# Values of two query blocks in one group, another order of the first transfers, and three output blocks per step in the last unit

## The chip, the core and the metric

The kernel runs on one core of one Trainium2 chip. The metric is the device time of the whole program in microseconds (us), the median of several executions. One further execution was recorded by the hardware profiler; all durations below are from it.

## What is computed

The reference is a three-layer transformer stack on one sequence of 512 tokens with a model width of 1024, all in float32. Cut to what matters here:

```python
# layer a: gMLP + attention over 256 memory rows, then a convolutional FFN
h = rmsnorm(x, a_norm1);  z = h @ a_w_in            # u | v | q_mem
u, vv, q_mem = gelu(z[:768]), gelu(z[768:1536]), z[1536:]
tok = u * spatial_gating(rmsnorm(vv))               # (GMLP blocks of 128)
x = x + concat(tok, memory_attention(q_mem, mem)) @ a_w_out
x = x + conv_ffn(rmsnorm(x))
# layer b: forgetting attention (12 heads of 64, causal, decay) + memory attention
x = x + concat(forgetting_attention(q, k, v, log_f_cum), memory_attention(...)) @ b_w_out
x = x + conv_ffn(rmsnorm(x))
# layer c: stick-breaking attention (8 heads) + differential attention (4 heads)
x = x + gate * (concat(sb_out, df_out) @ w_out_2)

# every softmax attention, for each block i of 128 queries and each head:
p = softmax(q_i @ k.T)          # logits, max, exp, normalisation
o_i = p @ v                     # needs p transposed: keys on the partitions
```

## The kernel before

Everything is kept transposed (features on the 128 partitions, 512 tokens on the free axis). Each large product is made of two float32r parts, high and low, so that one 128x128 weight block costs three TensorE matmuls: high x high, high x low, low x high (`blocks`, lines 380 to 398; `out_block`, lines 1808 to 1810). I call these three matmuls a block, and eight of them (one output tile) a job. A weight chunk comes by DMA into `raw` (two slots, SyncE's queue), ScalarE rounds it into `wh` (`split_hi`, line 300), VectorE subtracts to get `wl` (`split_lo`, line 306), and TensorE counts `w_used` when it is done with it. SyncE loads a chunk into a slot when VectorE has finished with the slot's last one (`w_lo`).

**The order of the work** is written out by hand on each engine, with semaphores between the engines. There is no scheduler.

**The start.** TensorE first runs 20 matmuls on a zeroed tile `warm` (line 1760). Then `value_group(0)` computes the first half of the v projection: for each of the eight 128-row slices k of x, twelve matmuls of 384 columns (lines 1700 to 1702), into four PSUM banks. Slice k needs `xh` and `xl` of that slice (ScalarE lines 444 and 445, VectorE lines 452 to 456; the squares for the norm are summed on the way, in `sq` and `acc`) and the weight chunk that holds slice k. The chunks of group 0 hold slices (0), (1), (2, 3, 4), (5, 6, 7) (`VSETS`). Ahead of slice 7 stand the sums of the squares over the partitions (`x_sums`, lines 1709 and 1715). SyncE issues par, chunk 0, x slice 0, chunk 1, x slice 1, x slices 2 and 3, chunk 2, x 4 and 5, x 6 and 7, chunk 3, and then constants and the memory rows.

**The softmax units.** Two heads share a unit. Ten units use `two_pe`, `two_act` and `two_dve`: `ma` 0 and 1 (memory attention of layer a), and in layer b `mb` 0, `fx` 0, `fx` 1, `mb` 1, `fx` 2 to 5 (`UNITS`). A unit has ten steps t (`pe_pairs`). In even steps TensorE does `logits(t/2)` of a query block (line 483, weights of 64 rows; for `fx` a mask matmul, line 540) and `turned` of the block before (line 547, transposes of the probabilities, 128 rows and columns). In each step it then does `between(t)`, a share of the projection jobs of the next unit: `FILL` gives 3, 3, 2, 2, 2, 3, 3, 0 jobs for the eight units of layer b, and the last unit of layer b does blocks of `b_out` instead. In steps 3, 5, 7, 9 it ends with `values(i)` for i = 0, 1, 2, 3 (line 559, weights of 64 columns). ScalarE's `copy` takes the transposes out of PSUM into `pta` or `ptb`, which has one half for each head. The first `values` of an `fx` unit also waits for `b_vn`: the values of this unit, transposed at t = 2 (line 436) and copied by ScalarE into `vnb`.

**The last unit** of the program (u = 7, differential attention) has its own copies of these steps (logits line 483, turns line 2020, values line 2032). No projection is left, so `between_last` puts blocks of the last product, `c_out`, there: `OUT_EARLY` lists 42 of them, and `OUT_FROM` gives how many are done by the start of each step: 2, 2, 2, 3, 2, 2, 2, 3, 2, 2. The others come after the unit.

Of the kernel before, what the change touches and what calls it, by code (L numbers as in the profile page):

```python
# [12 lines left out]
P = 128  # L13
D = 1024
S = 512
# [17 lines left out]
STAGES = [("front", 23, 14), ("a_out", 8, 8), ("a_f1", 44, 44), ("a_f2", 16, 8),  # L33
# [9 lines left out]
VSETS = (((0, 1), (1, 1), (2, 3), (5, 3)), ((0, 3), (3, 3), (6, 2)))  # L43
FRONT = ([("v", 0, i) for i in range(4)] + [("v", 1, i) for i in range(3)] +
# [3 lines left out]
FRONT_UNIT = [range(17, 20), range(20, 23)]  # L48
# [28 lines left out]
def build(nc, t, decay, out):  # L77
    with ExitStack() as ctx:
# [53 lines left out]
        minus = sb("minus", [P, 2 * P], F32R)  # L132
# [37 lines left out]
        pta = at("pta", [P, 2, MEM], F32, 24)  # L170
        vn = at("vn", [P, TT, TOKW], F32, 52)
        warm = at("warm", [P, S], BF16, 52)
# [12 lines left out]
        ptb = at("ptb", [P, 2, S], F32, 78)  # L185
# [11 lines left out]
        aws = at("aws", [P, 2, S], F32, 50)  # L197
        sgs = at("sgs", [P, S], F32, 56)
# [34 lines left out]
        x_hi, x_lo = sem("x_hi"), sem("x_lo")  # L233
        s_sum, s_root, s_r = sem("s_sum"), sem("s_root"), sem("s_r")
# [254 lines left out]
        def pe_pairs(logits, turned, values, between, behind_first=False):  # L489

            for t in range(PE_STEPS):
# [10 lines left out]
                if odd and i >= 1:  # L502
                    values(i - 1)
# [25 lines left out]
        def two_pe(pe, a, it, p, pt, q, k, v, nk, decayed, o_free, between, ready=None):  # L529
# [20 lines left out]
            def values(i):  # L550
# [6 lines left out]
                for b in range(last + 1):  # L557
                    for h in range(2):
                        mm = nc.tensor.matmul(ob[heads(h), i * P:(i + 1) * P], v(h, b), pt[:, h, b * P:(b + 1) * P],  # L559
                                              start=(b == 0), stop=(b == last))  # L560
# [126 lines left out]

        def front_width(n):
# [35 lines left out]
        def _(sp):  # L724
# [28 lines left out]
            def load_x(m):  # L753
                k = [i for i in range(KD) if XPART[i] == m]
                sp.dma_start(xt[:, k[0]:k[-1] + 1, :], t["x_t"][:, k[0]:k[-1] + 1, :]).then_inc(in_x[m], 16)
# [12 lines left out]
            for m in range(2):  # L768
                sp.dma_start(memt[:, 4 * m:4 * m + 4, :], t["mem_t"][:, 4 * m:4 * m + 4, :]).then_inc(in_mem[m], 16)
            load_front(4)  # L770
            sp.dma_start(wsnat[:, :, :], t["ws_t"]).then_inc(in_ws, 16)
            sp.dma_start(kf[:, 2 * P:NKEEP], t["k_tiles"][:, 2 * P:NKEEP]).then_inc(in_c, 16)
            load_front(5)
            sp.dma_start(biast[:, :, :], t["bs_t"]).then_inc(in_bi, 16)
            sp.dma_start(par[:, NROWS:], t["params"][:, NROWS:]).then_inc(in_c, 16)
            load_front(6)
            sp.dma_start(kb[:, :].bitcast(F32), t["k_bf16"]).then_inc(in_kb, 16)
            for n in range(7, len(FRONT)):
                load_front(n)
# [62 lines left out]
        def _(act):  # L842
# [8 lines left out]
            def value_gelu(g, b):  # L851
# [3 lines left out]
                else:  # L855
                    act.wait_ge(w_used, (4, 7)[g])
# [9 lines left out]

            table(EXP_LN_SET)
            act.wait_ge(in_par, 16)
            front_hi(0)
            for k in range(KD):  # L870
                x_hi_part(act, X0["a_in"], k, k % 2, col("a_norm1", k), xh, in_x[XPART[k]], 16)
                if k in (0, 2, 4):
                    front_hi(k // 2 + 1)
            front_hi(4)
            act.wait_ge(k_set, 1)
# [3 lines left out]
            front_hi(5)  # L879
# [8 lines left out]
            front_hi(6)  # L888
            front_hi(7)
            for b in range(TT):  # L890
                value_gelu(1, b)
            table(EXP_LN_SET)
            front_hi(8)
            factor(s_sum, 1, rmem[:, :], zb[0][:, :MEM], s_root, s_r)
            factor(c_sum, 1, sm[:, 56:58], zb[0][:, 260:262], c_root, c_rec)
            front_hi(9)
# [3 lines left out]
            for n in range(10, 19):  # L900
                front_hi(n)

            def behind_front(u):

                def f(t):
                    for n in FRONT_UNIT[u]:
                        if unit_end(u, n) + 1 == t and n < 21:
# [9 lines left out]
            def rest_front(u):  # L917
                mix_high(act, 6 + u, u, ob[:, :], att["ma"]["pv"], 8 * u + 8)
                for n in FRONT_UNIT[u]:
                    if unit_end(u, n) + 1 >= PE_STEPS - 1 and n < 21:  # L920
# [267 lines left out]
        def _(dve):  # L1188
# [34 lines left out]
            nc.vector.memset(warm[:, :], 0.0).then_inc(k_warm, 1)  # L1223
# [950 lines left out]
```

## Time and profile before

| | us |
|---|---|
| median of 3 executions | 1458.16 (1457.49 to 1461.1) |
| the profiled execution | 1456.96 |
| its span, first to last instruction | 1455.2 |
| TensorE matmuls busy | 1444.9 |
| VectorE busy | 961.2 |
| ScalarE busy | 670.1 |
| granted TensorE clock, mean | 1.00 of full |

A matmul's row gives its start and a modelled duration that overlaps the next matmul's start. So what a matmul costs is read from start to start: a 128x512 matmul of a block has a row of 0.39 us and the next one starts 0.23 us later. "Idle before" in brackets is time in which an engine ran nothing, with what ended it.

### The profile page before, as it was taken

To read this page: it belongs to the slowest core of one execution; us is meant where nothing else is said; L and a number is where in the kernel's file an instruction comes from. 1 tells how busy PE (TensorE), PEld (TensorE's weight loads), DVE (VectorE), ACT (ScalarE), POOL (GpSimd) and SP (SyncE) were. 2 spreads that over 40 slices of the span, in tenths; PEclk is the share of its full clock that TensorE was granted. 3 is DMA by queue.
4 is the path that set the end of the run, shared out by engine and by line. 5 is a ranking of instruction groups with operands and counts; after the bars stand their busy time and mean duration, and the time that the engine had idled before them with its cause. 6 is when DMAs were issued, how large, how long until landed. Compare 5 with 4: busy or idle time off the path is not lost.

```text
span 1455.2 us, 20045 instructions
## 1 busy us (share of the span) xinstructions
PE 1444.9 (99%) x7052; PEld 1152.1 (79%) x7052; DVE 961.2 (66%) x1581; ACT 670.1 (46%) x1104; POOL 41.2 (3%) x82
## 2 busy tenths in 40 slices
PE   9999999999999999999999999999999999999999
PEld 8977888888888887777778888888888877777777
DVE  5656777777766647555457777777677666666773
ACT  7435444444442234444454444444323366665661
POOL 0000000000001110000000000000111000000000
PEclk9999999999999999999999999999999999999999
DMA  6323222332247733212132323323676511112222
GB/s 226 129 89 117 73 88 100 101 98 90 101 143 232 241 107 116 74 59 88 59 102 67 106 86 101 101 88 117 202 243 232 166 51 59 58 58 73 73 74 87
DMA packets 44301, 162.66 MB, mean 112 GB/s; under 512 B 5060, under 2 KB 5700, under 8 KB 44240
## 3 DMA queue, kind: packets, MB, share of 16 engines
q1 hardware_dynamic: 33984, 126.70, 26.0%
q0 software_dynamic: 9104, 33.06, 6.8%
q10 hardware_dynamic: 1152, 2.10, 0.4%
q8 instruction: 37, 0.61, 0.2%
q14 instruction: 24, 0.20, 0.0%
HBM read 159.72 MB, written 2.12 MB: 111 GB/s over the span
## 4 chain that ended last, share of the span: by engine, by line
PE 95%; DVE 2%; ACT 1%; DMA 1%; issue 0%; SPq 0%; DVEq 0%; ACTq 0%
PE ps L380 17%; PE ps L382 17%; PE ps L381 17%; PE ps L396 6%; PE ps L398 6%; PE ps L397 6%; PE ps L1808 3%; PE ps L1810 3%; PE ps L1809 3%; PE ps L483 2%; PE ps L559 2%; PE ps L547 2%; PE ps L1986 2%; PE ps L1742 1%; PE ps L1744 1%; PE ps L1743 1%
## 5 line engine op out<-in xcount | busy, mean ns | idle before, releaser
L306 DVE TENSOR_TENSOR wl<-raw,wh 128x1024 fp32r<-128x1024 f32 (+3 forms) x198 | 253.7, 1281 | 122.9 <-ACT wh L300 122.8
L300 ACT CAST wh<-raw 128x1024 fp32r<-128x1024 f32 (+3 forms) x198 | 217.5, 1098 | 228.0 <-PE ps L382 194.8
L380 PE MATMUL ps<-xh,wh 128*128 128x512 f32 x720 | 281.1, 390 | 0.6 <-DVE hb L1366 0.6
L382 PE MATMUL ps<-xh,wl 128*128 128x512 f32 x720 | 280.1, 389 | 0.0
L381 PE MATMUL ps<-xl,wh 128*128 128x512 f32 x720 | 280.1, 389 | 0.0
L380 PEld LDWEIGHTS ps<-xh,wh 128*128 128x128 f32 x720 | 135.2, 188 | 29.5 <-issue 2.0
L381 PEld LDWEIGHTS ps<-xl,wh 128*128 128x128 f32 x720 | 135.2, 188 | 28.5 <-issue 0.5
L382 PEld LDWEIGHTS ps<-xh,wl 128*128 128x128 f32 x720 | 135.2, 188 | 28.3
L396 PE MATMUL ps<-xh,wh 128*128 128x512 f32 x344 | 144.8, 421 | 0.0
L380 PE MATMUL ps<-hth,wh 128*128 128x512 f32 x352 | 136.9, 389 | 0.0
L381 PE MATMUL ps<-htl,wh 128*128 128x512 f32 x352 | 136.9, 389 | 0.0
L382 PE MATMUL ps<-hth,wl 128*128 128x512 f32 x352 | 136.9, 389 | 0.0
L398 PE MATMUL ps<-xh,wl 128*128 128x512 f32 x344 | 134.8, 392 | 0.0
L397 PE MATMUL ps<-xl,wh 128*128 128x512 f32 x344 | 134.3, 390 | 0.0
L970 ACT CAST hth<-hid 128x512 f32 (+1 forms) x44 | 27.3, 621 | 136.6 <-DVE hid L1378 136.6
L963 ACT ACTIVATE ct<-hb,par 128x512 f32<-128x512 f32 x88 | 71.8, 816 | 34.2 <-DVE hb L1366 34.0
L1366 DVE TENSOR_TENSOR hb<-ps,rbc 128x512 f32<-128x512 f32 x88 | 60.5, 688 | 38.8 <-PE ps L382 38.7
L396 PEld LDWEIGHTS ps<-xh,wh 128*128 128x128 f32 x344 | 64.9, 189 | 15.4 <-issue 3.7
L381 PEld LDWEIGHTS ps<-htl,wh 128*128 128x128 f32 x352 | 66.1, 188 | 13.8
L380 PEld LDWEIGHTS ps<-hth,wh 128*128 128x128 f32 x352 | 66.1, 188 | 13.8
L382 PEld LDWEIGHTS ps<-hth,wl 128*128 128x128 f32 x352 | 66.1, 188 | 13.5
L398 PEld LDWEIGHTS ps<-xh,wl 128*128 128x128 f32 x344 | 64.6, 188 | 14.6
(300 smaller groups left out, 2347.7 us busy)
## 6 DMA issues: line engine op xcount, KB each, us to landing
raw<-w_a_f SPq DMA_DIRECT2D x44, 512.0 KB, 3.2
raw<-w_b_f SPq DMA_DIRECT2D x44, 512.0 KB, 3.2
row<-w_c_rows POOLq DMA_DIRECT2D x32, 512.0 KB, 4.6
row<-w_ada_rows POOLq DMA_DIRECT2D x24, 512.0 KB, 4.8
raw<-w_a_f SPq DMA_DIRECT2D x16, 704.0 KB, 4.0
raw<-w_b_f SPq DMA_DIRECT2D x16, 704.0 KB, 4.2
raw<-w_b_pair SPq DMA_DIRECT2D x18, 512.0 KB, 3.3
raw<-w_front SPq DMA_DIRECT2D x16, 512.0 KB, 3.2
```

The lines of the kernel that those rows point to most:

```text
L300: nc.scalar.copy(wh[:, s, :width], raw[:, s, :width]).then_inc(w_hi, 1)
L306: nc.vector.tensor_tensor(wl[:, s, :width], raw[:, s, :width], wh[:, s, :width].bitcast(F32), ALU.subtract).then_inc(w_lo, 1)
L380: nc.tensor.matmul(dst, a, h(k), start=(k == 0), stop=False)
L381: nc.tensor.matmul(dst, a, l(k), start=False, stop=False)
L382: mm = nc.tensor.matmul(dst, b, h(k), start=False, stop=(k == total - 1))
L396: nc.tensor.matmul(dst[:, :], a, h(r), start=(k == 0), stop=False)
L397: nc.tensor.matmul(dst[:, :], a, l(r), start=False, stop=False)
L398: mm = nc.tensor.matmul(dst[:, :], b, h(r), start=False, stop=(k == KD - 1))
L963: nc.scalar.activation(ct[:, l, :], hb[:, l, 2:], ACT.Identity, bias=w(3), scale=w(2)).then_inc(f_c0, 1)
L1366: nc.vector.tensor_tensor(hb[:, l, 2:], po[(J0[L + "_f1"] + l) % 2][:, :], rbc[:, :], ALU.mult).then_inc(po_free, 1)
L1808: nc.tensor.matmul(dst[:, :], a, MIX[0](r), start=(k == 0), stop=False)
L1809: nc.tensor.matmul(dst[:, :], a, MIX[1](r), start=False, stop=False)
```

## The change

Three things are changed.

1. `values` of query blocks 0 and 1 are both done at the end of step 5, those of 2 and 3 at the end of step 9 (`pv_at`), in the ten units of `two_pe`. The copied transposes have two buffers (`pta[i % 2]`, `ptb[i % 2]`), and `copy` waits for the values of two query blocks earlier. `minus` moves elsewhere in SBUF to make room.
2. The start: 9 matmuls on `warm` and not 20. x slice 0 is loaded from ScalarE's queue, chunk 0 is the first on SyncE's queue, then par, x slice 1, chunk 1; x slices 2 and 3 are issued when x slice 0 is there. The chunks hold slices (0), (1), (2), (3, 4), (5, 6, 7), one chunk more, so all numbers behind it rise by one. `xh` of slice 0 is made by VectorE. Slice 0's twelve matmuls are ordered by part (`first_products`). The squares are taken two slices at a time into `sqx` and added in pairs.
3. In the last unit three blocks of `c_out` are done in each step (`OUT_FROM`), 30 in all and not 22. Behind the unit 9 blocks, and not 8, stand ahead of the k = 7 blocks of the first four output tiles.

```diff
-STAGES = [("front", 23, 14), ...
+STAGES = [("front", 24, 14), ...
-VSETS = (((0, 1), (1, 1), (2, 3), (5, 3)), ((0, 3), (3, 3), (6, 2)))
+VSETS = (((0, 1), (1, 1), (2, 1), (3, 2), (5, 3)), ((0, 3), (3, 3), (6, 2)))
...
-        def pe_pairs(logits, turned, values, between, behind_first=False):
+        def pe_pairs(logits, turned, values, between, behind_first=False, pv_at={1: (0,), 2: (1,), 3: (2,), 4: (3,)}):
...
-                if odd and i >= 1:
-                    values(i - 1)
+                if odd and i in pv_at:
+                    for e in pv_at[i]:
+                        values(e)
...
-            pe_pairs(logits, turned, values, between)
+            pe_pairs(logits, turned, values, between, pv_at={2: (0, 1), 4: (2, 3)})
...
-                wait(act, a["pv"], 8 * it + s - 1)
-                nc.scalar.copy(pt[:, s % 2, :n], turn_bank(a, it, s)[:, :n]).then_inc(a["copy"], 1)
+                wait(act, a["pv"], 8 * it + s - 3)
+                nc.scalar.copy(pt[s // 2 % 2][:, s % 2, :n], turn_bank(a, it, s)[:, :n]).then_inc(a["copy"], 1)
...
+            load_front(0)
             sp.dma_start(par[:, :NROWS], t["params"][:, :NROWS]).then_inc(in_par, 16)
-            load_front(0)
-            load_x(0)
+            load_x(sp, 1)
             load_front(1)
-            load_x(1)
-            load_x(2)
+            sp.wait_ge(in_x[0], 16)
+            load_x(sp, 2)
             load_front(2)
-            load_x(3)
-            load_x(4)
             load_front(3)
+            load_x(sp, 3)
+            load_x(sp, 4)
+            load_front(4)
...
+            dve.wait_ge(in_par, 16)
+            dve.wait_ge(in_x[0], 16)
+            nc.vector.tensor_scalar(xh[:, 0, :], xt[:, 0, :], col("a_norm1", 0), None, ALU.mult).then_inc(x_hi, 1)
             front_lo(0)
...
+            first_add(1)
             front_lo(4)
+            first_lo(6)
+            first_lo(7)
+            first_add(2)
+            first_add(3)
+            dve.wait_ge(x_add, 3)
+            nc.vector.tensor_tensor(acc[:, :], sqx[:, 0, :], sqx[:, 1, :], ALU.add).then_inc(x_add, 1)
...
+            def first_products():
+                a, b = wh[:, 0, :VW], wl[:, 0, :VW]
+                for s_in, part, w in ((w_hi, xh, a), (w_lo, xh, b), (x_lo, xl, a)):
+                    pe.wait_ge(s_in, 1)
+                    pe.wait_ge(x_hi, 1)
+                    for i in range(TT):
+                        mm = nc.tensor.matmul(vbank[0][i][:, :VW], part[:, 0, i * P:(i + 1) * P], w,
+                                              start=(part is xh and w is a), stop=False)
+                mm.then_inc(w_used, 1)
...
-            for _ in range(20):
+            for _ in range(9):
                 nc.tensor.matmul(st[:, :], warm[:, 0:P], warm[:, :], start=True, stop=True)
...
-            OUT_FROM = [0, 2, 4, 6, 9, 11, 13, 15, 18, 20, 22]
+            OUT_FROM = [3 * t for t in range(PE_STEPS + 1)]
...
-            for i in range(23, 31):
+            for i in range(31, 40):
```

On ScalarE, at the start of the program before the change (`wh<-raw` is a weight chunk, `sq<-xt` and `xh<-xt` are the square and the high part of one x slice):

```order
1 L466 ACT_TABLE_LOAD
2 L300 CAST wh<-raw 128x384
3 L444 ACTIVATE sq<-xt 128x512
4 L445 ACTIVATE xh<-xt,par 128x512
5 L300 CAST wh<-raw 128x384
6 L444 ACTIVATE sq<-xt 128x512
7 L445 ACTIVATE xh<-xt,par 128x512
8 L444 ACTIVATE sq<-xt 128x512
9 L445 ACTIVATE xh<-xt,par 128x512
10 L300 CAST wh<-raw 128x1152
```

And after it (`sqx` takes the squares of two slices at once):

```order
1 L694 DMA xt<-x_t 128x512
2 L469 ACT_TABLE_LOAD
3 L303 CAST wh<-raw 128x384 x2
4 L448 ACTIVATE xh<-xt,par 128x512 x3
5 L303 CAST wh<-raw 128x384
6 L877 ACTIVATE sqx<-xt 128x1024
7 L303 CAST wh<-raw 128x768
8 L448 ACTIVATE xh<-xt,par 128x512 x2
9 L877 ACTIVATE sqx<-xt 128x1024
10 L303 CAST wh<-raw 128x1152
```

The high part of slice 0 has left ScalarE, both first chunks stand ahead of every x slice, and the squares stand behind the slices that they belong to.

On TensorE, in unit `fx` 1 of layer b before the change: the end of step 7, the start of step 8, and further down the end of step 9 with the logits of the next unit (L559 are the values, L547 the turns, L396 to L398 a block):

```order
1477 L398 MATMUL ps<-xbh,wl 128x512
1478 L559 MATMUL ps<-ptb,vnb 64x128 x6
1479 L547 MATMUL ps<-kf,pb 128x128 x8
1480 L396 MATMUL ps<-xbh,wh 128x512
...
1491 L398 MATMUL ps<-xbh,wl 128x512
1492 L559 MATMUL ps<-ptb,vnb 64x128 x8
1493 L483 MATMUL ps<-kmb,qmr 128x256 x2
```

And the same places after it (L563 the values, L551 the turns, L399 to L401 a block):

```order
1468 L401 MATMUL ps<-xbh,wl 128x512
1469 L551 MATMUL ps<-kf,pb 128x128 x8
1470 L399 MATMUL ps<-xbh,wh 128x512
...
1481 L401 MATMUL ps<-xbh,wl 128x512
1482 L563 MATMUL ps<-ptb_113,vnb 64x128 x6
1483 L563 MATMUL ps<-ptb_69,vnb 64x128 x8
1484 L486 MATMUL ps<-kmb,qmr 128x256 x2
```

The six values matmuls of query block 2 have moved from between a block and the turns to the end of the unit, where they stand directly ahead of those of block 3.

## Rows read from the trace of the kernel before

**Rows 1.** First part of the page: busy us, share of the span, instructions

```profile
PE 1444.9 (99%) x7052; PEld 1152.1 (79%) x7052; DVE 961.2 (66%) x1581; ACT 670.1 (46%) x1104; POOL 41.2 (3%) x82
```

**Rows 2.** Waits of PE, longest in total: us in total, times, longest

```profile
PE ps L2020 <- DVE pd L1661: 1.7, 2, 1.1
```

**Rows 3.** Timeline of PE and its weight loads, start: start us, us, engine, line

```profile
4.15 0.15 PEld L1760 LDWEIGHTS ps<-warm 128*128 128x128 bf16 x1 [0.28 <-issue]
4.49 1.39 PEld L1760 LDWEIGHTS ps<-warm 128*128 128x128 bf16 x7 [0.19 <-issue]
...
7.40 0.41 PE L1700 MATMUL ps<-wh,xh 128*128 128x384 f32 x1 [0.16 <-DVE xl L456]
...
12.49 0.44 PE L1700 MATMUL ps<-wh,xh 128*128 128x384 f32 x1 [0.29 <-DVE wl L306]
...
23.02 0.95 PE L1709 MATMUL ps<-kf,acc 128*128 128x1 f32 x8
```

**Rows 4.** Timeline of SP's queue, ACT and DVE, from the start

```profile
1.66 0.42 SPq L755 DMA_DIRECT2D xt<-x_t  x1
...
4.90 0.63 ACT L444 ACTIVATE sq<-xt 128x512 f32<-128x512 f32 x1 [0.48 <-DMA xt<-x_t]
...
6.51 0.74 DVE L456 SCALAR_TENSOR_TENSOR xl<-xt,par,xh 128x512 fp32r<-128x512 f32 x1
...
14.16 1.16 ACT L300 CAST wh<-raw 128x1152 fp32r<-128x1152 f32 x1 [0.90 <-DMA raw<-w_a_v]
...
15.36 1.36 DVE L306 TENSOR_TENSOR wl<-raw,wh 128x1152 fp32r<-128x1152 f32 x1 [0.20 <-ACT wh L300]
...
35.80 1.23 DVE L1234 TENSOR_TENSOR sqm<-sqm 128x1024 f32<-128x1024 f32 x1 [1.41 <-ACT sqm L886]
```

**Rows 5.** DMA view of the first 40 us: GB/s in each microsecond

```profile
GB/s 0 23 194 278 330 278 364 405 328 376 328 366 414 387 337 417 415 403 407 419 406 290 31 172 322 4 0 0 0 0 0 184 340 0 0 0 0 0 0 0
```

**Rows 6.** Timeline of PE in unit fx 1 of layer b

```profile
615.32 0.40 PE L398 MATMUL ps<-xh,wl 128*128 128x512 f32 x1
616.24 0.44 PE L559 MATMUL ps<-ptb,vnb 128*64 128x128 f32 x4 [0.52 <-issue]
616.61 0.92 PE L483 MATMUL ps<-kr,qr 64*128 64x384 f32 x4
...
620.78 1.13 PE L483 MATMUL ps<-kr,qr 64*128 64x512 f32 x4
...
624.47 0.39 PE L398 MATMUL ps<-xbh,wl 128*128 128x512 f32 x1
624.79 0.88 PE L559 MATMUL ps<-ptb,vnb 128*64 128x128 f32 x12
625.60 1.09 PE L547 MATMUL ps<-kf,pb 128*128 128x128 f32 x8
626.45 0.48 PE L396 MATMUL ps<-xbh,wh 128*128 128x512 f32 x1
```

**Rows 7.** Timeline of ACT and DVE in the same unit

```profile
615.58 0.56 ACT L1009 COPY vnb<-ps 128x512 f32<-128x512 f32 x1
```
```profile
625.26 0.48 DVE L608 TENSOR_SCALAR pb<-pb,sm 128x512 f32<-128x512 f32 x1
```

**Rows 8.** Timeline of PE in the last unit

```profile
1412.07 0.55 PE L2020 MATMUL ps<-kf,pd 128*128 128x128 f32 x3 [0.66 <-DVE pd L1661]
1412.37 0.48 PE L1808 MATMUL ps<-mixh,wh 128*128 128x512 f32 x1
...
1415.90 0.83 PE L2032 MATMUL ps<-ptd,vns 128*128 128x128 f32 x6
1417.80 0.66 PE L2020 MATMUL ps<-kf,pd 128*128 128x128 f32 x4 [1.07 <-DVE pd L1661]
```

**Rows 9.** Timeline of ACT and DVE in the last unit

```profile
1414.53 0.73 ACT L1159 ACTIVATE pd<-pd,sm 128x512 f32<-128x512 f32 x1
```
```profile
1416.99 0.75 DVE L1661 SCALAR_TENSOR_TENSOR pd<-pd,sm 128x512 f32<-128x512 f32 x1
```

More of the change, by code:

```diff
@@ L686, in leftover, with load_x @@
                     project(jobs[0] + j)
+        def load_x(eng, m):
+            k = [i for i in range(KD) if XPART[i] == m]
+            eng.dma_start(xt[:, k[0]:k[-1] + 1, :], t["x_t"][:, k[0]:k[-1] + 1, :]).then_inc(in_x[m], 16)
         def front_width(n):
@@ L865, in factor, with first_hi, first_squares @@
                 nc.scalar.activation(dst, dst, ACT.Exp, scale=-0.5).then_inc(s_out, 1)
+            def first_hi(k):
+                x_hi_part(act, X0["a_in"], k, k % 2, col("a_norm1", k), xh, in_x[XPART[k]], 16, square=False)
+            def first_squares(e):
+                p = (0, 1, 2, 1)[e]
+                nc.scalar.activation(sqx[:, 2 * p:2 * p + 2, :].rearrange("p a n -> p (a n)"),
+                                     xt[:, 2 * e:2 * e + 2, :].rearrange("p a n -> p (a n)"), ACT.Square).then_inc(x_sq, 1)
+            load_x(act, 0)
             table(EXP_LN_SET)
+            front_hi(0)
+            front_hi(1)
             act.wait_ge(in_par, 16)
[L869 to L873, printed above, removed]
-            front_hi(4)
+            act.wait_ge(x_hi, 1)
+            for k in (1, 2, 3):
+                first_hi(k)
+            front_hi(2)
+            first_squares(0)
+            front_hi(3)
+            first_hi(4)
+            first_hi(5)
+            first_squares(1)
+            front_hi(4)
+            first_hi(6)
+            first_hi(7)
+            first_squares(2)
+            act.wait_ge(x_add, 1)
+            first_squares(3)
+            front_hi(5)
             act.wait_ge(k_set, 1)
@@ L899, in _ @@
             factor(v_acc, 0, sm[:, 12:16], sm[:, 12:16], v_root, v_r, TOKW)
-            for n in range(10, 19):
+            for n in range(11, 20):
                 front_hi(n)
@@ L1248, in _ @@
             dve.wait_ge(s_r, 1)
-            for n in range(7, 17):
-                if n == 8:
+            for n in range(8, 18):
+                if n == 9:
                     dve.wait_ge(s_r, 2)
-                if n == 11:
+                if n == 12:
                     dve.wait_ge(c_rec, 2)
@@ L1255, in _ @@
                 front_lo(n + 2)
-                if n in (7, 9):
-                    for k in range(4 * (n == 9), 4 * (n == 9) + 4):
+                if n in (8, 10):
+                    for k in range(4 * (n == 10), 4 * (n == 10) + 4):
                         dve.wait_ge(m_hi, 8 + k + 1)
@@ L1688, in value_group @@
                     s = n % 2
+                    if n == 0:
+                        first_products()
+                        continue
                     pe.wait_ge(w_lo, n + 1)
@@ L1764, in _ @@
             value_group(1, mem_sums)
-            for n in range(7, 17):
-                if n < 9:
-                    pe.wait_ge(v_gelu, n - 2)
+            for n in range(8, 18):
+                if n < 10:
+                    pe.wait_ge(v_gelu, n - 3)
                 front_chunk(n)
@@ L2043, in _ @@
                 out_block("c_out", j, KD - 1)
-            for i in range(31, 42):
+            for i in range(40, 42):
                 out_block("c_out", *OUT_EARLY[i])
```

77 lines of the change are left out of this document (45 added, 32 removed).

## The prediction

> **What bounds the kernel now.** I read the page first: TensorE is busy 99% of the span, VectorE 66%, ScalarE 46% [rows 1]. So a change can only gain where TensorE starts late, waits, or pays something between two groups of matmuls that the busy figure hides. The view of TensorE's waits has little to give: the largest entry is 1.7 us in two waits of the last unit [rows 2]. What is hidden shows only in the timeline, read from start to start. There are three places, and the change touches each: the first 23 us [rows 3, 4], the joints of the attention units [rows 6], and the last unit [rows 8].
>
> **Values in pairs.** Read the end of step 7 in unit `fx` 1 [rows 6]. A block's last matmul starts at 624.47, and the values follow 0.32 later, where a block's matmuls follow each other every 0.23. The 12 values matmuls take 0.81 until the turns start. With 128 columns each at the pace that a 512-column matmul has (0.23 / 4, at best 0.053), 12 take 0.64. So 0.17 of the group is fixed. The group of 4 in step 3 takes 616.61 - 616.24 = 0.37 against 0.21: again 0.16 fixed. A values group uses 64 columns of weights, the logits 64 rows, all else 128 by 128: the fixed part is a change of that shape.
>
> - Step 3: the values go, the logits follow the block directly. The entry of 0.32 stays (it is then the logits'), 0.16 goes.
> - Step 7: the values go, and turns (128 by 128, as the block) follow the block. 0.17 goes, the entry falls by 0.09, and the turns' own 0.85 for 8 transposes probably loses some 0.05 of the same kind: 0.31.
> - Steps 5 and 9: the second group follows the first in the same shape: nothing.
>
> That is 0.47 a unit, and 4.7 us for ten units. The lower bound, if only the step-3 kind of saving holds at both places, is 3.2; the upper one, if a group's whole entry goes too (0.25 and 0.40), is 6.5. I take 4.7, the value read in the place itself.
>
> A second gain: in `fx` 1 the first values wait. From 615.32 to 616.24 are 0.92 us where 0.32 is normal, and 616.24 is just behind ScalarE's copy into `vnb`, which runs from 615.58 for 0.56 [rows 6, 7]. "Issue" in the brackets is thus a wait for `b_vn`. The other unit that begins with two jobs, `fx` 2, has the same shape. With the values in step 5 this copy is two steps old: 2 x 0.60 = 1.2 us gone.
>
> A new cost: what is removed was cover. The turns of step 8 need VectorE's normalisation of block 3, whose chain starts at logits(3) (620.78). The second of its two halves (two heads) ends at 625.26 + 0.48 = 625.74, 4.96 behind the logits [rows 6, 7]. TensorE would reach the turns now at 624.47 + 0.23 = 624.70, 3.92 behind the logits, and not at 625.60. The last four of the eight transposes wait until 625.8 and, at 0.1 each (0.85 / 8), end near 626.2, where without a wait all would be done at 625.5. That is 0.7 us of new wait. `fx` 2 has the same two jobs behind it, `mb` 1 too, with 256 columns and so a shorter chain; I put it at half, 0.4. Sum 1.8. In the units with three jobs a step holds 2.4 blocks and not 1.6; over two steps that is 1.1 us more cover (a block is 3 x 0.23), and 1.0 us is what is lacking. So I book nothing there, but it is close. The looser wait of `copy` (the second buffer) costs nothing, and step 4's turns lose 0.37 to 0.6 of cover, which in `fx` 1 the removed wait shows they have, since the turns stand behind the logits of 616.61 by 0.85 and more.
>
> Attention: -4.7 - 1.2 + 1.8 = **-4.1 us**. Bounds -6 (no new wait) and -2.
>
> **The start.** TensorE's first real product starts at 7.40 [rows 3]; it waited for `xl` of slice 0, whose chain began when x slice 0 came at 4.90 [rows 4]. Slice 0 was the third transfer on SyncE's queue, issued at 1.66, two slots of 0.42 behind the first [rows 4]; now it is the first on ScalarE's, 0.9 us earlier, so it comes near 4.0. VectorE makes `xh`, `wl` and `xl` in at most 0.74 each, the time of `xl`: all by 6.2, and `first_products` needs `xl` only for its last four matmuls, 8 x 0.175 behind its start. So TensorE starts it when the 9 warm matmuls end. Their weight loads are 0.43 apart up to 4.15, and from 4.49 seven fit in 1.39 [rows 3]; the ninth ends near 4.8. That alone would give 2.6 us. But the products must then be fed. The last chunk of group 0 (slices 5 to 7) came at 14.16 and its `wl` was done at 15.36 + 1.36 = 16.72 [rows 4]. What is transferred up to and with it is the same before and after: par (55 KB), eight x slices of 256 KB, eight slices of weights of 192 KB, 3639 KB or 3.73 MB. The stream reaches that sum at 13.1 us [rows 5], a microsecond before the cast, so it is the volume that sets the landing, and no order of issue changes it. Slice 5 can then not start before 16.8. Before, it ran near 12.49 + 3 x 2.1 = 18.8 (slices 2 to 6 and nothing else lie between 12.49 and 23.02: 60 matmuls at 0.175). The gain is 2.0, and `x_sums` comes at 16.8 + 4.2 = 21.0 and not 23.0. VectorE's sum of squares ends there as well: behind `wl` at 16.7 come two `xl` (1.5), two adds of 1024 columns (1.23 each) and one of 512 (about 0.7), near 21.3, or 21.0 with the overlap of successive rows. Everything behind hangs on TensorE's progress and moves with it.
>
> The Trainium skill ("DMA: Bandwidth & Descriptors", Specifications) gives 435 GB/s as the ceiling of the transfers into SBUF; the busiest microsecond here shows 419 [rows 5], so the trace comes near it, but the mean from 2 to 13 us is 333. By that rule the chunk could land 2 us earlier, VectorE's chain would set `x_sums`, and the gain would be 2.8.
>
> Start: **-2.0 us**. Bounds -2.8 (the chunk lands 0.8 earlier) and -0.5 (one of the now tighter steps, chunk 2 behind x slices 2 and 3 above all, costs 1.5).
>
> **The last unit.** TensorE waits 0.66 before the turns of block 2 and 1.07 before those of block 3 [rows 8]. Both are for VectorE's normalisation, and TensorE's work behind the unit is the same whatever stands inside. A block takes 0.70 (five between 1412.37 and 1415.90). By step 6 five more blocks have been done, of which two lie between logits(2) and the turns of block 2: 1.4 against a wait of 0.66. Between the turns of block 2 and of block 3 there are six blocks, not five. The chain behind logits(3) is set by ScalarE, whose exponential starts at 1414.53 and leads to `pd` at 1416.99 + 0.75 = 1417.74 [rows 9]. It starts when ScalarE has done its list for the step, and this list moves by two blocks (1.4), TensorE by six (4.2) less the 0.66 won: 1.4 - 4.2 + 0.66 = -2.1 against 1.07. Both waits go: **-1.7 us**. The new waits that are possible are for the weights of output tiles 2, 3 and 4 (made in steps 3, 5, 7, read first in steps 4, 7, 9) and for the mixed row of unit 6, read from step 6 on. By their distances they are met with 1 us and more to spare, since TensorE is the one that comes later. Bounds -1.8 and 0.
>
> **The sum.** -4.1 - 2.0 - 1.7 = **-7.8 us**. The profiled execution took 1456.96 and would take 1449.2; it lies 1.2 below the median of the runs, 1458.16, so I predict 1450.4.
>
> **Rivals.**
>
> 1. *New waits eat the attention's gain.* If the normalisation is late by 0.7 us at step 8 in all ten units, attention is -4.7 - 1.2 + 7 = +1.1, and the total -2.6: 1455.6. For it: the three-job units have only about 0.1 us to spare by my count. Against: memory units have chains of 256 columns, and the first `fx` units of three jobs show no wait now. Chance 0.12.
> 2. *The start doesn't move.* TensorE starts early but stands for the chunks, and gains nothing by slice 5: -5.8, 1452.4. For it: 3639 KB is a fixed volume. Against: before, slice 5 ran 2 us behind its weights. Chance 0.08.
> 3. *Slower: the slow pace comes back.* The weight loads show that the array runs at half pace (1.2 GHz) up to the eighth warm matmul, then at 2.4 [rows 3]. Nine matmuls leave one or none at the fast pace. If the clock rises later, or falls in a gap while slices 1 and 2 wait, a product of 384 columns costs 0.32 and not 0.17; from 53 of the 96 products of group 0 on this outweighs 7.8 us, and with all 96 the time is 1458.16 - 7.8 + 14.4 = 1464.8. Against: a gap of 0.5 us ahead of 12.49 brought no slow product, and 12 products a slice keep the array busy. The Trainium skill ("TensorE: Matmul & The Clock Gate", Part 1) says the slow state is the default, that activity releases it, and that the moment varies by some 0.5 us from run to run. A shift of 0.5 us would make three products slow, 0.5 us. Chance 0.03.
> 4. *The edit of the last unit does nothing* (the chains move with the blocks): -6.1, 1452.1. Chance 0.05.
>
> The forecast keeps 0.72. A measurement of this kernel can tell about 0.3% (4.4 us) from no change. Faster by more than that: the forecast and rivals 2 and 4 less their outliers, 0.82; within 0.3%: rival 1 and a part of the rest, 0.14; slower: rival 3 and what I don't see, 0.04. The range: the best bounds sum to -10.6, the worst to -2.5; I take 1447.0 to 1455.0.
>
> **What would show it.** In the new trace: the first product near 4.8; slice 5 near 16.8 and the sums of squares near 21.0; no entry for values in steps 3 and 7, and turns directly behind a block; in `fx` 1 and 2 a wait of TensorE for `pb` at step 8 of about 0.5 that wasn't there, and none for `vnb`; no wait for `pd` in the last unit. The prediction is wrong if such waits for `pb` stand in all `fx` units, if slice 5 starts later than 17.5, or if 384-column products 0.32 apart stand behind the warm ones.

## The result and the profile after

The changed kernel takes 1450.09 us (median of 5 runs, 1449.13 to 1451.27), the kernel before 1458.16 (1457.49 to 1461.1, also of 5). The ratio is 0.9944, with a 95% interval of 0.9932 to 0.9955: 8.1 us faster, where 7.8 were forecast. The profiled execution took 1451.27, the longest of the five, with a span of 1449.5; that of before, 1456.96, is below each of those five. So the two traces differ by 5.7 us only. What is missing to 8.1 lies at the start and in what follows from it, as the table below shows.

The head of the page and the waits of TensorE (us in total, times, longest us), to be held against [rows 1, 2]:

```profile
PE 1438.8 (99%) x7041; PEld 1151.6 (79%) x7041; DVE 961.8 (66%) x1579; ACT 669.5 (46%) x1100; POOL 41.0 (3%) x82
```
```profile
PE ps L1753 <- DVE wl L309: 2.2, 2, 1.3
...
PE ps L551 <- DVE pb L612: 0.7, 2, 0.3
PE ps L399 <- DVE wl L309: 0.7, 1, 0.7
...
PE ps L486 <- ACT pb L579: 0.6, 2, 0.3
PE ps L1806 <- DVE wl L309: 0.4, 1, 0.4
```

The wait for `pd`, 1.7 us before, is gone. Two waits for `pb` at the turns are new, as forecast. But 2.2 us of waits for weights in group 0 (L1753) and 0.7 in a unit of stage `sb` (L399) are new as well, and neither was booked.

The start of TensorE after (start us, us, engine, line; against [rows 3]):

```profile
4.98 0.94 PE L1766 MATMUL ps<-wh,xh 128*128 128x384 f32 x4 [0.31 <-DVE xh L1261]
...
7.54 0.41 PE L1753 MATMUL ps<-wh,xh 128*128 128x384 f32 x1 [0.23 <-DVE xl L459]
10.78 0.44 PE L1753 MATMUL ps<-wh,xh 128*128 128x384 f32 x1 [0.90 <-DVE wl L309]
18.57 0.44 PE L1753 MATMUL ps<-wh,xh 128*128 128x384 f32 x1 [1.27 <-DVE wl L309]
23.18 1.02 PE L1772 MATMUL ps<-kf,acc 128*128 128x1 f32 x8
```

The first product comes at 4.98 (4.8 was forecast), 2.4 earlier than before. Yet slice 5 starts at 18.57, behind 1.27 of waiting, and the sums at 23.18: in this execution nothing is left of the head start. The queue of SyncE, ScalarE and VectorE show why (against [rows 4]), and the DMA view of the first 40 us shows where the transfers dip (against [rows 5]):

```profile
10.76 0.33 SPq L759 DMA_DIRECT2D raw<-w_a_v  x1
```
```profile
15.97 1.16 ACT L303 CAST wh<-raw 128x1152 fp32r<-128x1152 f32 x1 [0.59 <-DMA raw<-w_a_v]
```
```profile
17.16 1.36 DVE L309 TENSOR_TENSOR wl<-raw,wh 128x1152 fp32r<-128x1152 f32 x1 [0.52 <-ACT wh L303]
```
```profile
GB/s 0 39 217 385 331 138 331 285 257 366 379 325 189 355 282 258 324 410 424 385 415 399 370 278 61 120 351 21 0 0 0 106 381 37 0 0 0 0 0 0
```

The load of the last chunk is issued at 10.76, because it waits for the slot that chunk 2 leaves, and VectorE ends chunk 2 at 10.7. The microseconds from 5, from 8 and from 12 move 138, 257 and 189 GB/s, where before none from 3 to 14 us was under 278; the one from 12 follows on a stretch from 7.9 to 10.76 in which SyncE issues nothing. By 14 us 3.60 MB had come, and before 4.07. This is one execution: in `mixed`, a kernel below with the same code up to the first unit, 3.83 MB had come by then.

In unit `fx` 1 (against [rows 6]) the values of blocks 0 and 1 are one group of 12, and the turns of step 8 come straight behind a block, but late:

```profile
616.61 0.40 PE L401 MATMUL ps<-xbh,wl 128*128 128x512 f32 x1
616.94 0.88 PE L563 MATMUL ps<-ptb,vnb 128*64 128x128 f32 x12
617.75 1.13 PE L486 MATMUL ps<-kr,qr 64*128 64x512 f32 x4
...
621.44 0.39 PE L401 MATMUL ps<-xbh,wl 128*128 128x512 f32 x1
622.17 1.25 PE L551 MATMUL ps<-kf,pb 128*128 128x128 f32 x8 [0.35 <-DVE pb L612]
623.18 0.48 PE L399 MATMUL ps<-xbh,wh 128*128 128x512 f32 x1
```

Nothing waits for `vnb` any more: the values start 0.33 behind their block, and not 0.92. From the block to the end of the turns are 0.73 + 1.01 = 1.74; in the units of three jobs, where nothing waits, it is 0.23 + 0.79 = 1.02. So the new wait costs 0.72, twice the 0.35 that its row shows. A row counts idle time from the modelled end of the block's last matmul, 0.16 behind the point where the next one would have started (0.39 against 0.23): that makes 0.50 ahead of the group. The other 0.22 lies inside the group, whose second four transposes wait for VectorE's second half, and the merged row hides it. In the last unit (against [rows 8]) both turns follow without a wait:

```profile
1411.08 0.55 PE L2084 MATMUL ps<-kf,pd 128*128 128x128 f32 x3
...
1415.37 0.39 PE L1874 MATMUL ps<-mixh,wl 128*128 128x512 f32 x1
1415.60 0.83 PE L2096 MATMUL ps<-ptd,vns 128*128 128x128 f32 x6
1416.26 0.60 PE L2084 MATMUL ps<-kf,pd 128*128 128x128 f32 x4
```

### The profile page after: what moved, and what is told of

Its sections match the earlier page's. It is cut to its first block, busy times and chain, and to the rows that moved or that the text cites. A ratio compares the mean times of both kernels' runs of the same rounds, so it can differ in the third digit from the quotient of the medians.

```text
span 1449.5 us, 20006 instructions
## 1 busy us (share of the span) xinstructions
PE 1438.8 (99%) x7041; PEld 1151.6 (79%) x7041; DVE 961.8 (66%) x1579; ACT 669.5 (46%) x1100; POOL 41.0 (3%) x82
## 4 chain that ended last, share of the span: by engine, by line
PE 93%; DVE 4%; DMA 2%; ACT 1%; issue 1%; POOL 0%; ACTq 0%; DVEq 0%; POOLq 0%
PE ps L383 17%; PE ps L384 17%; PE ps L385 17%; PE ps L399 5%; PE ps L401 5%; PE ps L400 5%; PE ps L1872 3%; PE ps L1874 3%; PE ps L1873 3%; PE ps L486 3%; PE ps L563 2%; PE ps L2050 1%; PE ps L551 1%; PE ps L1806 1%; PE ps L1808 1%; DVE wl L309 1%
## 5 line engine op out<-in xcount | busy, mean ns | idle before, releaser
L399 PE MATMUL ps<-xh,wh 128*128 128x512 f32 x344 | 144.5, 420 | 0.7 <-DVE wl L309 0.7
L401 PE MATMUL ps<-xh,wl 128*128 128x512 f32 x344 | 134.6, 391 | 0.0
L399 PEld LDWEIGHTS ps<-xh,wh 128*128 128x128 f32 x344 | 64.9, 189 | 16.0 <-issue 4.4
L401 PEld LDWEIGHTS ps<-xh,wl 128*128 128x128 f32 x344 | 64.6, 188 | 14.3
```

Source lines behind the costliest of these rows:

```text
L399: nc.tensor.matmul(dst[:, :], a, h(r), start=(k == 0), stop=False)
L401: mm = nc.tensor.matmul(dst[:, :], b, h(r), start=False, stop=(k == KD - 1))
```

## The experiments

Ten other kernels and the changed one once more ran in three groups, each group on one chip with the kernel before beside it (medians 1458.51 for `pairs_only`, `out_only`, `start_only` and `no_start`; 1457.66 for `warm20`, `mem_later`, `early2` and `mixed`; 1458.2 for `step3_only`, `after_again` and `best`). The theory was the sum of the prediction, with the start corrected: the issue of the last chunk's load sets slice 5. To tell parts apart below the resolution of the times, I cut every profiled execution at the same instructions. "Sums" is the start of `x_sums`, "first unit" that of `ma` 0. All in us:

| kernel | median | up to sums | sums to first unit | two `ma` units | `a_out` to `b_qm` | eight layer-b units | to last unit | last unit to end |
|---|---|---|---|---|---|---|---|---|
| before | 1458.16 | 23.02 | 58.42 | 46.92 | 431.98 | 188.23 | 648.47 | 58.16 |
| pairs_only | 1453.93 | 23.95 | 58.23 | 45.95 | 431.98 | 185.30 | 648.34 | 58.15 |
| out_only | 1456.09 | 23.61 | 58.77 | 46.91 | 432.00 | 188.25 | 648.45 | 56.11 |
| no_start | 1452.36 | 23.78 | 58.38 | 45.95 | 431.99 | 185.29 | 648.43 | 56.18 |
| step3_only | 1455.2 | 23.71 | 58.47 | 46.53 | 432.02 | 186.17 | 648.41 | 58.19 |
| start_only | 1456.17 | 22.09 | 56.99 | 46.94 | 432.25 | 188.26 | 648.85 | 58.12 |
| after | 1450.09 | 23.18 | 57.72 | 45.92 | 432.23 | 185.35 | 648.98 | 56.12 |
| after_again | 1450.6 | 23.83 | 56.98 | 45.96 | 432.27 | 185.31 | 649.66 | 56.09 |
| warm20 | 1451.35 | 23.36 | 57.92 | 45.95 | 432.21 | 185.31 | 649.15 | 56.10 |
| mem_later | 1450.26 | 22.77 | 56.96 | 45.92 | 432.21 | 185.31 | 649.21 | 56.12 |
| early2 | 1449.85 | 21.86 | 56.96 | 45.92 | 432.21 | 185.29 | 649.71 | 56.05 |
| mixed | 1448.46 | 21.52 | 56.99 | 45.94 | 432.23 | 184.34 | 649.08 | 56.10 |
| best | 1448.84 | 22.77 | 56.97 | 45.92 | 432.24 | 184.34 | 648.72 | 56.04 |

Five of these traces have the old start and eight the new one. Four of the eight (`start_only`, `after`, `after_again`, `mixed`) have the same code up to the first unit. Where nothing was changed, the two `ma` units, the layer-b units and the last unit repeat within 0.15 us from kernel to kernel. The piece up to the sums doesn't, with either start (23.02 to 23.95, 21.52 to 23.83), nor does, with the new start, the piece up to the last unit.

**One part each.** Three kernels make one part of the change each, and one makes all but the start.

```diff
 # against before
-            pe_pairs(logits, turned, values, between)
+            pe_pairs(logits, turned, values, between, pv_at={2: (0, 1), 4: (2, 3)})
...
-                wait(act, a["pv"], 8 * it + s - 1)
-                nc.scalar.copy(pt[:, s % 2, :n], turn_bank(a, it, s)[:, :n]).then_inc(a["copy"], 1)
+                wait(act, a["pv"], 8 * it + s - 3)
+                nc.scalar.copy(pt[s // 2 % 2][:, s % 2, :n], turn_bank(a, it, s)[:, :n]).then_inc(a["copy"], 1)
...
```

> The kernel before with the values of two query blocks in one group, and nothing else. Theory A (the joints of the attention units pay as read from the two traces: 0.47 us a unit gone, two waits for vnb of 0.6 gone, new waits for pb and the exponentials of 2.1 in the three units with two jobs): -3.8 us against the kernel before. Theory B (the whole difference of the medians that the start does not explain, 2.4 us, sits in the attention too): -6 us or more.

1453.93, ratio 0.9974 (0.9965 to 0.9983). By the medians 4.6 us, with 2.5 to 5.1 as its interval: theory B's 6 or more is out. The segments say -0.97 and -2.93, -3.9 together: theory A's figure. Cut at the first logits of each unit, `fx` 1 loses 0.33 and `fx` 2 0.30, `mb` 1 takes 0.15 more, and the five other layer-b units lose 0.47 to 0.51 each.

```diff
 # against before
-            OUT_FROM = [0, 2, 4, 6, 9, 11, 13, 15, 18, 20, 22]
+            OUT_FROM = [3 * t for t in range(PE_STEPS + 1)]
...
-            out_block("c_out", *OUT_EARLY[22])
+            out_block("c_out", *OUT_EARLY[30])
...
```

> The kernel before with three output blocks in every step of the last unit, and nothing else. Theory A: the two waits for pd of 1.7 us go and nothing replaces them: -1.5 to -1.7 us. Rival: the chains of ScalarE and VectorE move with the blocks and the waits stay in part: 0 to -0.7 us.

1456.09, ratio 0.9985 (0.9976 to 0.9994), 2.4 us by the medians. The last unit loses 2.05 us, more than theory A's 1.5 to 1.7, and the rival is out.

```diff
 # against after
-            pe_pairs(logits, turned, values, between, pv_at={2: (0, 1), 4: (2, 3)})
+            pe_pairs(logits, turned, values, between, pv_at={1: (0,), 2: (1,), 3: (2,), 4: (3,)})
...
-            OUT_FROM = [3 * t for t in range(PE_STEPS + 1)]
+            OUT_FROM = [0, 2, 4, 6, 9, 11, 13, 15, 18, 20, 22]
...
```

> The kernel before with the new start alone (values and output blocks in the old order, the second buffer is kept). Theory A (the profiled execution is typical: slices 5 to 7 wait for their weight chunk, whose load is issued 3 us later than before): -0.5 us, slice 5 starts near 18.6 us. Theory B (the profiled execution was a bad one, the volume of the transfers sets the landing): -2.0 us or more, slice 5 near 16.8 us.

1456.17, ratio 0.9983 (0.9974 to 0.9992), 2.3 us under before by the medians, with 1.2 to 3.8 as its interval. That is theory B's time and not theory A's. Slice 5 starts at 17.48, between the two figures, so neither reason is confirmed.

The diffs of `pairs_only` and `out_only` together:

> The changed kernel without the new start: values in pairs and three output blocks a step on the kernel before. If the parts add up: -5.4 us (-3.8 and -1.6) against the kernel before, and 0.5 us (theory A) or 2.5 us (theory B) slower than the changed kernel, which measured -8.1.

1452.36, ratio 0.9966 (0.9952 to 0.9979): 6.1 us for the two other parts, and with the 8.1 of the whole change 2.0 for the start. The three parts alone give 4.6 + 2.4 + 2.3 = 9.3 by the medians, each with about 1.4 us to either side, against 8.1 for the whole; no interaction can be told from that.

**Where in the attention.** Only the values of blocks 0 and 1 are put together:

```diff
 # against pairs_only
-            pe_pairs(logits, turned, values, between, pv_at={2: (0, 1), 4: (2, 3)})
+            pe_pairs(logits, turned, values, between, pv_at={2: (0, 1), 3: (2,), 4: (3,)})
```

> The kernel before with the second buffer and with only the first two values groups put together: the values of blocks 0 and 1 stand in step 5, those of blocks 2 and 3 stay in steps 7 and 9. This splits the attention's gain by place. Theory (0.16 us for each values group that goes between two blocks of logits, another 0.31 at step 7, two waits of 0.60 for vnb that go with step 3, and new waits of 0.7 before the turns of step 8 that come from the removal at step 7 alone): the ma units lose 2 x 0.16 = 0.3 us (46.9 to 46.6), the layer-b units 8 x 0.16 + 1.2 = 2.5 less a wait of 0.3 to 0.4 for an exponential in mb 1 (188.2 to 186.1), no wait for pb at step 8 in fx 1 and fx 2; about 2.4 us under the kernel before, 1455.5. Rival (the fixed price of a change of shape is the same at both places, 0.24 each): ma units 46.4 and layer b 185.5, 3.3 us under before. A second rival (the vnb wait only moves): layer b 187.3.

1455.2, ratio 0.9981 (0.9972 to 0.999); `ma` 46.53, layer b 186.17: the theory said 46.6 and 186.1, the rival with equal shares 46.4 and 185.5, the second rival 187.3. The time, 3.0 us under before, can't tell them apart (2.4 and 3.3 were expected); the segments can. The units `fx` 1 and `fx` 2 lose 0.73 and 0.71 and the five others 0.13 to 0.21 (`mb` 1 takes 0.21 more): so each wait for `vnb` was worth some 0.55. Step 3 is worth (46.92 - 46.53) / 2 = 0.20 in a unit, step 7 (46.53 - 45.95) / 2 = 0.29; 0.16 and 0.31 were predicted. In `fx` 1 of this kernel the turns of step 8 have no wait, and stand behind the values again:

```profile
623.75 0.39 PE L399 MATMUL ps<-xbh,wl 128*128 128x512 f32 x1
624.07 0.88 PE L561 MATMUL ps<-ptb,vnb 128*64 128x128 f32 x12
624.88 1.09 PE L549 MATMUL ps<-kf,pb 128*128 128x128 f32 x8
625.73 0.48 PE L397 MATMUL ps<-xbh,wh 128*128 128x512 f32 x1
```

So the wait for `pb` comes from the removal at step 7 alone: what was taken out there was cover.

That a joint is paid for the change of shape, and not for any change from one group to another, can be read from groups that don't change it. In after, eight turns (128 by 128) directly behind a block:

```profile
600.70 0.39 PE L401 MATMUL ps<-xh,wl 128*128 128x512 f32 x1
600.94 1.03 PE L551 MATMUL ps<-kf,pb 128*128 128x128 f32 x8
601.73 0.48 PE L399 MATMUL ps<-xh,wh 128*128 128x512 f32 x1
```

They start 0.23 behind the block's matmul, as a matmul of the block would, and take 0.79; behind values of 64 columns they take 0.85. The values of the last unit use all 128 columns: at 1415.60 they too start 0.23 behind a block, and the six of them take 0.66 to the turns, 0.11 each, the pace of the turns themselves. No kernel changed the shape alone, so this stands on rows and not on an experiment.

The next kernel puts the values back as cover only in the three units that lack it, `fx` 1 and 2 and `mb` 1:

```diff
+            PV_AT = {0: {2: (0, 1), 4: (2, 3)}, 2: {2: (0, 1), 3: (2,), 4: (3,)},
+                     3: {1: (0,), 2: (1,), 3: (2,), 4: (3,)}, 4: {2: (0, 1), 3: (2,), 4: (3,)}}
...
-                        between_pe(u), (b_vn, it + 1))
+                        between_pe(u), (b_vn, it + 1), PV_AT.get(u, PV_AT[0]))
```

> The changed kernel where the three units with two jobs behind them keep a separate values group: fx 1 and fx 2 in step 7, mb 1 in steps 3 and 7 as before the change. Theory (removing a group took away cover, and the waits for pb and for the exponential that came cost more than the joints saved there): the two waits for pb of 0.35 and the one for the exponential of 0.3 at these units go, 0.41 us gained in each fx unit and 0.2 in mb 1, 1.0 us in all: 1449.1. Rival (the turns take as long as they do for other reasons than the wait): 1.3 us slower, since the joints come back (0.31 + 0.31 + 0.47) and nothing else changes.

1448.46, ratio 0.9936 (0.9922 to 0.9949), and the layer-b units take 184.34, 1.01 less than after, as the theory says: a wait of 0.72 goes for a joint of 0.29 that comes back, twice, and 0.17 in `mb` 1. The rival, 1.3 slower, is out.

**The start.** Twenty warm matmuls again with everything else as changed, so that TensorE starts as late as before:

```diff
-            for _ in range(9):
+            for _ in range(20):
```

> The changed kernel with 20 warm matmuls, and not 9, so that the first product starts near 7.3 us again and not at 5.0. Theory A (what ends the start last is the weight chunk of slices 5 to 7, whose products began at 17.5 and 18.6 us in two executions; slices 0 to 4 take 10.4 us and would end at 17.8): 0 to 0.5 us slower than the changed kernel, 1450.1 to 1450.6. Theory B (each microsecond of an earlier first product is gained): 2.3 us slower, 1452.4.

1451.35, ratio 0.9952 (0.9938 to 0.9965): 1.3 above after, 0.7 above after_again, with intervals as wide as that. It lies above theory A's range and below theory B's figure, and the times don't decide. In its trace the first product starts at 7.39, slices 0 to 4 run without a gap, the last matmul of slice 4 starts at 18.00, and slice 5 waits until 18.76 for the last chunk. So here, as in after (18.57), it is the chunk that sets slice 5. With the earliest chunk of the four executions of after's start (16.90 in mixed) TensorE would have come 1.3 later than the chunk: 20 warm matmuls cost something in such a draw and nothing in this one.

Two kernels move what could hold the last chunk. In one the mem tiles' two loads stand behind the next weights' load and not ahead of it, in the other chunk 2 is treated ahead of x slice 3, so that its slot is free earlier:

```diff
 # mem_later: on SyncE
+            load_front(5)
             for m in range(2):
                 sp.dma_start(memt[:, 4 * m:4 * m + 4, :], t["mem_t"][:, 4 * m:4 * m + 4, :]).then_inc(in_mem[m], 16)
-            load_front(5)
```
```diff
 # early2; the same for first_lo on VectorE
-            for k in (1, 2, 3):
-                first_hi(k)
+            first_hi(1)
+            first_hi(2)
             front_hi(2)
+            first_hi(3)
```

> The changed kernel with the load of the memory rows (1 MB, needed after 28 us) issued behind the first chunk of group 1 and not ahead of it. Theory A (the chunk of slices 5 to 7 lands 5.2 us after its issue because kf and the memory rows share the transfers with it): it lands up to 1.5 us earlier, slice 5 near 17 us, and the time is 0.5 to 1 us under the changed kernel's 1450.1. Rival (it lands late because it is issued at 10.8, when VectorE has done chunk 2, and behind x slices 4 to 7): no difference.

1450.26, ratio 0.9943 (0.993 to 0.9957): no difference by time. The chunk is cast at 15.56, 4.9 behind its issue, and slice 5 starts at 18.16, within what after's own start does (16.90 to 19.23).

> The changed kernel with chunk 2 rounded and subtracted between slices 2 and 3 on ScalarE and VectorE, not behind slice 3. Theory (issue time counts: the load of slices 5 to 7 waits for VectorE to be done with chunk 2, at 10.8 us): it is issued 0.6 us earlier, slice 2 starts 0.6 earlier on TensorE, slice 5 0.5 earlier, 0.5 us faster than 1450.1. Rival (the volume of the transfers counts): slice 2 earlier, slice 5 as before, no difference.

1449.85, ratio 0.9944 (0.9931 to 0.9958), equal by time. In the trace the load is issued at 10.08, 0.7 earlier than in after, and slice 5 starts at 17.25. That is no proof for the theory: mixed, with the load issued at 10.34 by after's own order, has slice 5 at 16.90.

The changed kernel once more, and then the edits of `mixed`, `mem_later` and `early2` together:

> The changed kernel once more, on the chip of the other runs of this call. Theory: the attention, the last unit and layer a's feed-forward agree with its first trace within 0.1 us (45.9, 185.3, 56.1), and only the time up to the first unit differs, within 79 to 82 us, since there the landing of the transfers decides. Rival (the first trace's 80.9 us of start is this order's own): again 80.9 within 0.2.

1450.6, ratio 0.9949 (0.9936 to 0.9963), and a start of 80.81, within the theory's 79 to 82 and at the rival's number, 80.9 within 0.2, too. But start_only and mixed, whose code up to here is the same, have 79.08 and 78.51, so the rival is out, and the theory's range was too narrow below. The agreement with after is a coincidence of two pieces that moved against each other: the sums came at 23.83, not 23.18, and the way from there to the first unit took 56.98, not 57.72.

> The changed kernel with the three edits together that looked best alone: the values of blocks 2 and 3 apart again in the units where their removal brought a wait, the fifth weights chunk's load issued ahead of the mem tiles, and x slice 3 treated behind chunk 2 on ScalarE and VectorE. Theory (the issue of the last chunk's load, gated by chunk 2's two halves, sets slice 5): the load is issued near 10.1 us, slice 5 starts at 16.9 to 17.5, the layer-b units take 184.3, and the time is 1.6 to 2.4 us under the changed kernel of the same call, about 1448. Rival (the volume sets it): slice 5 as in the changed kernel, and only the 1.0 us of the attention.

1448.84, ratio 0.994 (0.9926 to 0.9953): 1.8 under after_again, no better than mixed alone. The time lies in the theory's 1.6 to 2.4, but not for its reason. The load was issued at 9.99, earliest of all, and yet it was cast at 15.55 only, and slice 5 started at 18.16, where 16.9 to 17.5 was expected. That was a miss for the theory:

```profile
9.99 0.33 SPq L759 DMA_DIRECT2D raw<-w_a_v  x1
```
```profile
15.55 1.16 ACT L303 CAST wh<-raw 128x1152 fp32r<-128x1152 f32 x1 [0.31 <-DMA raw<-w_a_v]
```

All thirteen traces side by side give what stands of it. With the old order the last chunk's load is issued at 7.59 to 7.76 and cast at 14.16 to 14.74, within 0.6 us. With the new order it is issued at 9.99 to 11.06 and cast at 14.30 to 16.63, 4.0 to 5.9 behind the issue, and slice 5 follows at 16.90 to 19.23. With the old order this chunk never mattered: its low part was done by 16.7 to 17.4, and TensorE came to slice 5 at 18.9 to 19.8. What set the old start was the chunk of slices 2 to 4, cast at 9.84 to 10.84, whose low part TensorE waits for in all five traces, until 12.49 to 13.44; the trace of before that the prediction read was the earliest of them. With the new order TensorE waits for the last chunk in seven of eight traces, and in the eighth (mixed) it comes just with it: the earliest landings are as early as before, and the others up to 2 us later. Which issue time goes with which landing is not regular enough to call the issue the only cause, and what makes up the spread is open.

**The wait that nobody looked at.** The table shows where the start's gain is: 1.0 of it up to the sums (23.61 on average with the old start, 22.66 for the four executions that start as after does), and 1.3 between the sums and the first unit (58.45 against 57.17). The second part was in nobody's sum. It is one wait, at the first block of `kb` 0 of layer b in the front. Before, TensorE, and ScalarE ahead of it:

```profile
68.34 0.39 PE L1742 MATMUL ps<-memhb,wh 128*128 128x256 f32 x1 [1.13 <-DVE wl L306]
```
```profile
65.91 1.05 ACT L300 CAST wh<-raw 128x1024 fp32r<-128x1024 f32 x1 [3.32 <-DMA raw<-w_front]
```
```profile
raw<-w_front SPq DMA_DIRECT2D x1, 512.0 KB, 4.9
```

The last row is the issue at 60.99 in the DMA view of 60 to 62 us: 4.9 us from issue to landing, where its neighbours take 3.1 to 3.4. After_again has the same load, issued at 61.76, in 3.4, and ScalarE casts it at 65.17, 0.7 earlier than before, though its sums were 0.8 later:

```profile
raw<-w_front SPq DMA_DIRECT2D x1, 512.0 KB, 3.4
```
```profile
65.17 1.05 ACT L303 CAST wh<-raw 128x1024 fp32r<-128x1024 f32 x1 [1.82 <-DMA raw<-w_front]
```

In the five traces with the old start a load issued near 61.5 takes 4.7 to 5.2, and TensorE waits 0.9 to 1.5 for it. In the eight with the new start two have such a load (4.5 in warm20; 4.1 and 4.3 for the next ones in after), with waits of 0.7 and 0.4, and six have none. Why the load is slow with the old start isn't known; no kernel moved it. The row of an instruction load (q8, one packet) stands within 3.1 us behind the issue in all thirteen traces, but also where the load took 3.1 to 3.4; whether it has part in it wasn't tried.

**What is given back.** With the new start the stretch `a_out` to `b_qm` takes 0.25 more in all eight traces, and the stretch up to the last unit 0.3 to 1.3 more. Of the latter 0.4 to 0.7 is one wait in a unit of `sb`, in all eight (0 to 0.15 with the old start); here after:

```profile
1172.23 0.47 PE L399 MATMUL ps<-xh,wh 128*128 128x512 f32 x1 [0.68 <-DVE wl L309]
```

VectorE's chain ahead of it is held by its dot product, which waits for a row that GpSimd loads; in after_again

```profile
1160.49 1.22 DVE L1373 SCALAR_TENSOR_TENSOR row<-row,vec 128x1024 f32<-128x1024 f32 x1 [2.56 <-DMA row<-w_c_rows]
```

and with the old start, in no_start, at 1160.28 behind 1.02 of waiting, though TensorE is 1.0 us later there. The last two or three such loads take at most 3.5 in no_start and before, up to 4.4 in after_again. TensorE comes earlier and the row doesn't. What sets the landing of the row, and where the 0.25 is, stays open.

## Why the prediction was right, and where not

**Joints, -4.7: right.** 0.97 in two `ma` units is 0.485 a unit, against 0.47; over ten units 4.85. The split by place was right too (0.20 and 0.29 against 0.16 and 0.31).

**The waits for `vnb`, -1.2: right.** step3_only shows them by themselves, 0.56 in `fx` 1 and 0.54 in `fx` 2. The eight layer-b units gained 2.93; with 8 x 0.485 = 3.88 of joints and 1.1 of these waits, some 2.1 were given to new waits.

**New waits, +1.8: right in place, low by 0.3.** 0.72 in `fx` 1 and again in `fx` 2, against 0.7 each; in `mb` 1 0.67 against 0.4. There the prediction had only the turns (they cost 0.27); the logits at 634.41 wait for ScalarE's exponential besides, for 0.40. The values of step 3 had been its cover. The other units have no new wait, as booked, and lose 0.47 to 0.51 each, so rival 1 is out.

**The last unit, -1.7: right, low by 0.35.** Both waits went and nothing replaced them. The term that was too small is the price of the two waits: the sum took the idle time of the rows, 0.66 and 1.07. From start to start, in [rows 8], the values of block 2 and the wait last from 1415.90 to 1417.80, 1.90, and after from 1415.60 to 1416.26, 0.66: the wait had cost 1.24. The logits ahead of the first wait give 0.73 where 0.66 stood idle. That makes 1.97 of the 2.05. Rival 4 is out.

**The start, -2.0: the size right by luck, the step wrong.** The step that failed is the sentence that the volume sets the landing and no order of issue changes it. 3639 KB are the same, but the load of the last chunk was issued 3 us later, and the chunk was cast at 15.97 and not 14.16. By the prediction's own bound (slice 5 not later than 17.5) the step is refuted: 18.57. Only three of the eight new-start executions met the bound, mixed best with 16.90, where 16.8 was forecast: there the chunk was cast at 14.30, as before. The Trainium skill ("DMA: Bandwidth & Descriptors", Specifications) gives a ceiling of 435 GB/s, and the prediction's estimate from it had the chunk 2 us earlier (its rows give 2.6). The trace of after doesn't bear that out: its best microsecond up to 14 us moves 385 GB/s, and the mean from 2 to 13 us is 291, where it was 333.

Two more steps failed. The gain was counted from the trace of before, whose sums came at 23.02, 0.6 earlier than the average of the old start. And from slice 5 to the sums the prediction had 4.2; it is 4.6 in all eight traces of the new order, since TensorE then waits for VectorE's last addition of the squares, which the prediction saw at 21.3 or 21.0 and booked at 21.0.

What made the medians agree with 2.0 is partly another place: on average over the profiled executions 1.0 by the sums and 1.3 by the wait in the front, less 0.25 and 0.7 given back, which makes 1.3; by the medians it is 2.0 to 2.3. The four profiled executions lie 0.3 above their medians on average, those with the old start 0.4 below; with that it is 2.0, but no single trace shows it. Rival 2 ("the start doesn't move") is what the profiled execution of after shows up to the sums, and the medians don't.

**The clock, rival 3: no.** The first four products, right behind the ninth warm matmul, are 0.195 apart, the rest 0.17: none at 0.32, so they run at the level of 2.4 GHz. The granted clock doesn't tell here: it reads 1.00 from the first microsecond on, also where the warm matmuls are 0.43 apart.

## What to carry to other kernels

A group of matmuls that uses another part of the array (64 columns or 64 rows of weights) between two groups alike cost 0.20 to 0.29 us here beyond its columns. So put such groups together, but only where what they covered is still covered: look for the wait behind the place where the group stood, and leave it where there is one. Price a wait from start to start and not by the idle time in its row (0.72 for 0.35, 1.24 for 1.07). When the order of loads is changed, follow the slot of each load to the engine that frees it, and not only the bytes ahead of it. And a difference at the start has to be judged over several executions, of the kernel before too: one trace of it was 0.6 us from the average.

## What the runs showed of the hardware that was not expected

- A load of 576 KB in the busy start was cast 4.0 to 5.9 us behind its issue in the eight executions of the new order. The four with the same code up to there had 4.0, 4.3, 5.2 and 5.9.
- Between loads of 512 KB that take 3.1 to 3.4 us, the one issued near 61.5 us took 4.7 to 5.2 in all five traces of the old start.
- Turns behind a block, both 128 by 128, cost nothing for the change of group: they start 0.23 behind it and are 0.11 apart. Values of 64 columns start 0.32 behind the block, and the turns behind them take 0.85 and not 0.79.
- The idle time in a row of TensorE is less than what the wait costs: two waits cost 0.72 for 0.35 and 0.40 for 0.32, a longer one 1.24 for 1.07. This is in the way the row is made, and not a time of the chip's own.
